# Moving the last page step, the head pick and its copy inside the attention loop of a decode-and-prompt kernel

## The reference

```
h = rms_norm(x) @ w_in                      # queries, keys, values, gates of two head groups
prompt: o = window + selected + compressed attention (8 heads), causal 512 x 512
        d = softmax(q1 k1) v - lam * softmax(q2 k2) v     (8 differential heads)
decode: the same over 4096 cached tokens; differential values: a @ v_all, 8 heads x 64,
        with v_all gathered page by page (32 pages of 128 tokens for each of 8 sequences)
        selected attention over 16 blocks of 64 tokens for each sequence and key head
y = x + concat(o * silu(z_n), rms_norm(d) * silu(z_d)) @ w_out
```

## Time and profile before

| | value |
|---|---|
| median of three runs | 860.74 us |
| own time of the profiled execution | 861.4 us |
| span of its trace | 859.5 us |
| PE busy | 785.2 us, 91% |
| DVE busy | 449.6 us, 52% |
| ACT busy | 190.3 us, 22% |
| moved by DMA | 220.67 MB, mean 257 GB/s |

### The profile page before, as it was taken

How to read it: one execution, slowest core, us unless ns; L and a number is a source line. 1 busy time by engine, 2 the same in 40 slices (tenths; PEclk the granted TensorE clock), 3 DMA queues, 4 the chain that set the end, 5 groups by cost and what they waited for, 6 DMA issues and landing times.

```text
span 859.5 us, 14940 instructions
## 1 busy us (share of the span) xinstructions
PE 785.2 (91%) x4891; PEld 383.9 (45%) x4891; DVE 449.6 (52%) x972; ACT 190.3 (22%) x492; POOL 19.6 (2%) x38
## 2 busy tenths in 40 slices
PE   6999999899989989999999999898888878887997
PEld 2475535354444435444535663343433333345443
DVE  2133243427304348778536546777585493784923
ACT  1311120002101202122213403443242241344000
POOL 0000000000000100010002000000000000000000
PEclk9999999999999979999999986999798698887999
DMA  9976797969897699978674169998698888872011
GB/s 342 307 252 211 272 339 239 382 223 376 263 338 248 244 374 346 361 254 334 240 266 148 40 229 311 341 342 266 197 280 271 265 260 295 317 299 96 1 49 51
DMA packets 137768, 220.67 MB, mean 257 GB/s; under 512 B 17481, under 2 KB 66802, under 8 KB 136346
## 3 DMA queue, kind: packets, MB, share of 16 engines
q1 hardware_dynamic: 114826, 196.45, 66.4%
q10 hardware_dynamic: 20528, 14.27, 5.5%
q0 software_dynamic: 2336, 8.99, 3.1%
HBM read 213.77 MB, written 10.04 MB: 260 GB/s over the span
## 4 chain that ended last, share of the span: by engine, by line
PE 62%; SPq 15%; DVE 9%; DMA 8%; issue 4%; ACT 1%; DVEq 0%
PE banks L595 14%; PE banks L617 13%; SPq L387 10%; PE banks L1042 6%; PE banks L852 5%; PE banks L563 4%; DMA proj<-in_cmp_cache 3%; PE banks L631 3%; DMA ring<-in_dk_cache 3%; PE banks L882 2%; DVE att L1732 2%; SPq L405 2%; DMA ring<-in_dv_cache 2%; PE banks L898 2%; SPq L382 2%
## 5 line engine op out<-in xcount | busy, mean ns | idle before, releaser
L617 PE MATMUL banks<-ring,xt 128*128 128x512 f32 (+1 forms) x448 | 188.9, 575 | 0.0
L617 PEld LDWEIGHTS banks<-ring,xt 128*128 128x128 f32 x448 | 84.3, 193 | 93.9 <-issue 90.9
L595 PE MATMUL banks<-proj,wide 128*64 128x256 f32 x896 | 102.9, 392 | 1.7 <-DMA proj<-in_cmp_cache 1.7
L1272 ACT ACTIVATE wide<-banks,att 128x128 f32<-128x128 f32 (+3 forms) x128 | 66.4, 523 | 160.0 <-DVE att L1732 152.4
L852 PE MATMUL banks<-ring,small 128*32 128x512 f32 x512 | 80.3, 718 | 8.9 <-DMA ring<-in_dv_cache 8.8
L595 PEld LDWEIGHTS banks<-proj,wide 128*64 128x64 f32 x896 | 67.7, 141 | 38.8 <-DMA proj<-in_cmp_cache 6.7
L631 PE MATMUL banks<-ring,small 128*32 128x512 f32 x512 | 65.3, 623 | 15.5 <-DMA ring<-in_dk_cache 15.5
L1457 DVE TENSOR_SCALAR small<-small 128x510 f32<-128x510 f32 x8 | 3.4, 426 | 142.8 <-ACT small L1111 128.0
L1096 ACT ACTIVATE proj<-banks,x_rs 128x512 f32<-128x512 f32 (+1 forms) x32 | 21.2, 663 | 200.7 <-PE banks L617 162.4
L898 PE MATMUL banks<-consts,wide 128*128 128x128 f32 x240 | 46.5, 322 | 20.2 <-DVE xt L1756 9.7
L882 PE MATMUL banks<-proj 32*128 32x128 f32 (+7 forms) x256 | 61.5, 562 | 0.0
(11 more groups left out here) (342 smaller groups left out, 806.0 us busy)
## 6 DMA issues: line engine op xcount, KB each, us to landing
ring<-in_dk_cache SPq DMA_DIRECT2D x256, 256.0 KB, 6.1
ring<-in_dv_cache SPq DMA_DIRECT2D x256, 256.0 KB, 4.2
proj<-in_cmp_cache SPq DMA_DIRECT2D x144, 128.0 KB, 4.0
ring<-in_w_in SPq DMA_DIRECT2D x6, 2048.0 KB, 11.0
proj<-in_cmp_cache ACTq DMA_DIRECT2D x80, 128.0 KB, 5.8
ring<-in_x_nat SPq DMA_DIRECT2D x2, 2048.0 KB
ring<-in_cmp_cache SPq DMA_DIRECT2D x32, 128.0 KB, 3.1
ring<-in_w_out SPq DMA_DIRECT2D x1, 4096.0 KB, 12.4
```

The lines of the kernel that those rows point to most:

```text
L595: last = mm(to, w1[:, kv, half, lp, :], rows[:, kv, g, lp, :, :, :], start=lp + half == 0, stop=lp == LP - 1 and half == 1, tile_position= ...
L617: last = mm(banks[:, 3 + n % 2, 0:width(c)], xt[:, k, P * t:P * t + P], w_ring[:, c % 2, k, 0:width(c)], start=k == 0, stop=k == KC - 1)
L1272: last = A(e_slot(j, c)[:, 0:n], banks[:, 2 * (j % 2) + c, 0:n], ACT.Exp, bias=row_max[:, j % 4, c:c + 1], accum_out=row_sum[:, j % 4, c:c ...
```

## The change

On PE the v step 8b+7 no longer goes ahead of the scores of j = 8b+3 but takes the usual place, behind `turn`. The pick moves behind `turn` of j = 8b+4, right in front of v step 8b+8. On DVE `mask_v` moves from behind `mask_max` of j = 8b+3 to the front of j = 8b+4. `keep_v` moves from ACT to DVE, behind `mask_max` of j = 8b+4, as a `tensor_copy`. Nothing is computed otherwise.

```diff
 PE
-                early = j < DUOS and j % 8 == V_EARLY - 1
-                if early:
-                    v_step(j + V_EARLY)
                 if j < DUOS:
                     scores_of(j)
-                if j < DUOS and j % 8 == V_EARLY:
-                    pick(j // 8)
...
                 if 2 <= j < DUOS + 2:
                     turn(j - 2)
-                if not early and j + V_EARLY < 64:
+                if j < DUOS and j % 8 == V_EARLY:
+                    pick(j // 8)
+                if j + V_EARLY < 64:
                     v_step(j + V_EARLY)
 ACT
-            def keep_v(b):
-                act.wait_ge(s("v_picked"), b + 1)
-                A(o_diff[:, :, b], banks[:, 7, 0:4], ACT.Copy).then_inc(s("o_diff_kept"), 1)
-                if j < DUOS and j % 8 == V_EARLY:
-                    keep_v(j // 8)
 DVE
+            def keep_v(b):
+                dve.wait_ge(s("v_picked"), b + 1)
+                V.tensor_copy(o_diff[:, :, b], banks[:, 7, 0:4]).then_inc(s("o_diff_kept"), 1)
...
+                if j < DUOS and j % 8 == V_EARLY:
+                    mask_v(j // 8)
                 if j < DUOS:
                     mask_max(j)
-                if j < DUOS and j % 8 == V_EARLY - 1:
-                    mask_v(j // 8)
+                if j < DUOS and j % 8 == V_EARLY:
+                    keep_v(j // 8)
                 if 1 <= j < DUOS + 1:
                     scale(j - 1)
```

## The result

The change makes the kernel slower. Twenty runs of each give a median of 867.28 us after and 859.09 us before; the ratio is 1.011 with a 95% interval of 1.0084 to 1.0138, so between 7.2 and 11.9 us are lost, where +3.3 us was forecast and 861.0 to 866.8 us was the range. The runs of one kernel spread more than the three shown first suggested: 852.55 to 866.25 us before, 861.39 to 874.01 us after. The profiled execution of after took 865.28 us, its span is 863.4 us.

A forecast was written before the change was run, and what follows sets the result against it. DVE bounds the wide handovers, PE the narrow ones, sel_place's loads 2 and 6, SP's stream the stretch between. Terms -0.5, -1.2, +3.5, 0, +2.4, -0.9 sum to +3.3 us: 864.0 us, range 861.0 to 866.8 us.

The forecast's parts named there:

- Handover 2: At j = 19 and 20, mask_v queued behind sel_place delays the selected scores; +3.5 us, bounds +1.1 and +7.3.
- handover 1: At j = 11, v step 15 no longer precedes the scores, DVE starts earlier; -1.2 us, bounds -2.05 to -0.2.
- Handover 6: At the second selected attention, the same delayed path as at handover 2; +2.4 us.
- From there to v step 53: After handover 2, SP's stream passes the delay on; other changes go into PE's 2.54 us wait; 0 us.
- B: Rival: delays before v step 53 vanish in PE's 2.54 us wait there; 862.2 us, chance 0.11.
- Handover 0: At the first handover, PE's 0.76 us wait for mask_v goes, 0.28 us for the copy comes; -0.5 us.
- Handover 7: At the last handover, v step 63 leaves its place ahead of scores 59, DVE starts earlier; -0.9 us.
- ACT (0): ACT loses a 0.18 us copy in eight places where it was waiting for PE; 0 us.
- A: Rival: PE stays longer at half clock after new idle at handovers 2 and 6; 866.3 us, chance 0.14.
- C: Rival: selected blocks land before DVE reaches sel_place, which then no longer holds mask_v; 859.5 us, chance 0.11.
- D: Rival: C, and earlier scores free SP, so page waits shrink by some 2.5 us; 857.0 us, chance 0.07.

The follow-up runs named there:

- e5: The changed kernel with twelve unused matmuls filling PE's idle ahead of the picks of handovers 2 and 6; 1.0058 of before, 865.30 us to 862.45.
- e3: The kernel before with the changed order at all handovers except 2 and 6; 0.9985 of before, 862.68 us.
- e9: The kernel before with the changed order at handover 2 alone; 1.005 of before, 864.22 us to 861.28.
- e11: e8 with the selected scores put ahead of the v step at j = 20 and 52; 0.9994 of before, 860.77 us to 861.28.
- e6: The changed kernel with, at handovers 2 and 6, mask_v ahead of sel_place and the copy on ACT; 1.0017 of before, 861.96 us to 862.45.
- e8: e3 with ACT's block loads ended three j earlier in both halves; 0.9977 of before, 858.20 us to 862.45.
- e4: The changed kernel with only the copy back on ACT, at all eight handovers; 1.008 of before, 867.40 us to 860.87.
- e1: The changed kernel with only mask_v back ahead of sel_place at handovers 2 and 6; 1.0031 of before, 863.63 us to 860.87.
- e2: The kernel before with the changed order at handovers 2 and 6 alone; 1.0093 of before, 867.90 us to 860.87.
- e10: The kernel before with the changed order at handover 6 alone; 1.0063 of before, 867.98 us.
- e7: The changed kernel with ACT's 39 block loads in j = 2 to 15 instead of 2 to 18; 1.0087 of before, 866.57 us to 862.45.

## Why the prediction was wrong in size

The direction and the mechanism were right: `mask_v` and `keep_v` are caught behind the waiting `sel_place`, and the selected scores start late. The forecast was +3.3 us and the measurement +8.2 to +9.4 us.

*Handover 2 (+3.5).* This step failed in its size, and it is the term that most of the error comes from. It "take[s] +3.5, between the two" prices of the v step, and it takes the pick at 1.05 us, a row of handover 1, where PE had been busy until just before. At handover 2 PE had been idle for 3.46 us, and the pick took 1.87 us, the v step 1.68 us to the start of the next work. The lag grew by 4.69 us where the forecast had 3.5, and the selected scores themselves took 4.74 instead of 4.49 us. The piece of the loop grew by +5.0 us. The prediction had written that half clock follows waits, and then used it for one of the three operations, and by half. The term's upper end (+7.3) held it, but the forecast's own upper bound (+5.9) was added up with +3.85 for this term and with the pick at 1.05 us, and the range was built on that. The Trainium skill (TensorE: Matmul & The Clock Gate, Part 1) calls the reduced clock the default, and rows of after agree: 0.50 was granted at both handovers, behind 3.46 and 4.37 us of idle, and e5, without the idle, had its 1.05 us.

*Handover 6 (+2.4).* Failed for the same reason and a second one. It was computed against the lag of 1.49 us of the earlier trace rows, which was one execution's. e3, e9, e11, e6 and e8 had 0.40 to 0.69 us there with the old order. The lag grew by 3.6 us against that one execution and by 4.6 us against the usual one; the piece grew by +4.7 us, of which the next piece gave back 1.4, though that piece alone spreads from 18.1 to 21.4 us in the old order. Net +3.3 us. Had I not taken a single row as typical, this term would have been about that of handover 2.

*From there to v step 53 (0).* Right in what it says of SP, and it was what decided between the forecast and B. The means of the piece from 21 to 50 are equal to 0.1 us whether handover 2 is late or not (single profiles lie between 118.7 and 122.2 us), so the +5.0 us is passed on, as far as this spread lets one see, and SP's wait for the first selected values is again 5.5 us in after:

```profile
SPq L401 <- PE banks L973: 5.5, 1, 5.5
```

The wait for v step 53 was 0.61 us in after, not 2.54; PE waited at other v steps instead (four between 669 and 706 us). Where in this stretch PE waits for pages changes from one execution to the next.

*Handover 0 (-0.5) and handover 1 (-1.2).* Right in place, wrong in what becomes of it. The rows gave -1.16 us at handover 1, and the pieces -1.7 and -1.0 us. But from 0 to 18 the two orders differ by 0.0 us: the pieces behind each handover are longer by 1.9 and 0.7 us. The timeline of PE in after shows on what. Four v steps in a row behind handover 0 waited for their pages, where before had no such wait until 549 us:

```profile
530.28 1.06 PE L852 MATMUL banks<-ring,small 128*32 128x512 f32 x8 [0.58 <-DMA ring<-in_dv_cache]
534.01 1.07 PE L852 MATMUL banks<-ring,small 128*32 128x512 f32 x8 [1.67 <-DMA ring<-in_dv_cache]
537.46 1.06 PE L852 MATMUL banks<-ring,small 128*32 128x512 f32 x8 [1.38 <-DMA ring<-in_dv_cache]
540.97 1.94 PE L852 MATMUL banks<-ring,small 128*32 128x512 f32 x8 [0.58 <-DMA ring<-in_dv_cache]
```

These 4.2 us of waits lie in the piece that grew. e4 has the same four (533 to 543 us, 3.95 us in all). The other profiles agree: where the piece from 2 to 5 took 10.1 us or more (before, e1, e2, e9), no v step from 5 to 10 waited for pages; where it took 9.9 us or less, they waited 1.3 to 4.4 us in all, in e10 too, which has the old order there. The prediction followed SP's stream only between the two selected attentions; in the first eighteen j it is a bound as well, and what PE gains there it can wait for pages later. By these means the term of -1.7 us should have been 0, another 1.7 us of the error. But the two columns for 0 to 18 reach from 58.1 to 61.4 and from 56.8 to 61.8 us, so a gain of about 1 us could hide in them.

*Handover 7 (-0.9).* Right: -0.9 us in the piece from 58 to 61. SP has issued the last value pages by then (at 740 us in before, where the v step of this handover comes at 755 us).

*ACT (0).* Not contradicted: e4 puts the copies back, and its time cannot be told from after's.

The terms as measured: 0.0 + 5.0 + 0.0 + 3.3 - 0.9 = +7.4 us, for +3.3 forecast. Of the 4.1 us between them, 1.5 come from handover 2, 0.9 from handover 6 and 1.7 from handovers 0 and 1. The whole loops give +6.2 or +7.7 us, depending on whether e7 and e11 are counted.

*The rivals.* A (866.3 us, given 0.14) was the nearest: its place and cause were right, and its price of +4.65 us for handover 2 is near the 4.69 us by which the lag grew. That nearness is luck: 4.65 is a lag of 3.85 us and 0.8 us for longer selected scores, with the pick still at full clock, while the runs had 0.82 us more in the pick and 0.25 us more in the selected scores (4.74 less 4.49). It shared the wrong base of handover 6 and the gains of 0 and 1. B fell by e9. C (the landing is not last) fell twice: `sel_place` waited 2.50 and 3.40 us in after, and e7, where it did not wait, kept a lag of 4.87 us and lost 2.1 us from 18 to 21 against the old order's 18.0 us. C had priced `mask_v` behind `sel_place` at 0.8 us once the loads are early. D fell with it.

What stays open: the 2 to 3 us between the loop's +6.2 or +7.7 us and the ratio's +9.4, and whether putting `sel_scores` first (e11) really shortens the loop.

## What to carry to other kernels

Before moving an instruction on an engine that works in order, list what on that engine waits for a transfer, and keep ahead of it everything that another engine needs: here the selected scores start 0.4 us behind the landing when the hand-off chain is done before the wait, and 5.1 us when it is queued behind it. Price a hand-off chain that starts behind an idle TensorE (3.46 and 4.37 us here) at half clock throughout, small matmuls too. Take a slack or a lag from one execution only with the spread that similar places show, and ask of every gain on PE whether the stream of its pages can follow.

## What the runs showed of the hardware

The pick, eight matmuls with 128x128 weights and one column each, is nearly all weight loading: PEld was busy for 1.78 of its 1.87 us at 0.50 of the clock, and for 0.97 of 1.05 us at full clock (e3). So weight loads slow down with the clock (1.78 to 0.97) about as the multiplications of a v step do (1.93 to 1.06).

Filling an idle stretch with unused matmuls gave time back: in e5 the lag fell from 5.09 to 3.45 us, and the pieces from 22.2 and 23.9 to 19.3 and 19.7 us. It still lost to keeping the order (1.0058 against before).

Executions of one kernel on one core spread by 1.6% (852.55 to 866.25 us over 20 runs of before). The longer executions have the lower granted clock: of 24 executions of after the eight shortest (861.39 to 866.25 us) had 0.938 on average, the eight longest (869.08 to 874.01 us) 0.928. Three runs within 0.13% of each other had suggested a bound of 0.2% for no change; with 9 to 20 runs of a kernel the intervals are 0.3 to 0.5% to either side.
